# Three expert gathers on one Trainium2 core: down and up rows fetched as one 8 KB row, with weights made row by row

## The reference, cut to what matters

```
def _peer(h, w_pq, peer_keys, peer_down, peer_up):
    q = (h @ w_pq).reshape(B, L, 8, 2, 128)
    s = einsum("blhpd,hpkd->blhpk", q, peer_keys)          # 128 keys per half
    sv, si = lax.top_k(s, 16)
    cand = sv[..., 0, :, None] + sv[..., 1, None, :]       # 256 candidates a head
    top_s, pos = lax.top_k(cand.reshape(..., 256), 16)
    eidx = ...                                             # one of 16384 experts
    gate = softmax(top_s)
    # per block of 128 tokens: 8 heads x 16 = 128 experts a token
    a   = einsum("tkd,td->tk", peer_down[eidx], h)
    act = gate * gelu(a)
    out = einsum("tk,tkd->td", act, peer_up[eidx])
```

## Time and profile before

| | us |
|---|---|
| median of 3 runs | 4169.66 |
| lowest, highest | 4167.23, 4174.44 |
| span of the profiled execution | 4362.9 |
| first gather in it (four tiles) | 447 to 2089 |
| second gather (two tiles) | 2232 to 3065 |
| third gather (two tiles) | 3605 to 4353 |

### The profile page before, as it was taken

How to read it: one execution, slowest core, us unless ns; L and a number is a source line. 1 busy time by engine, 2 the same in 40 slices (tenths; PEclk the granted TensorE clock), 3 DMA queues, 4 the chain that set the end, 5 groups by cost and what they waited for, 6 DMA issues and landing times.

```text
span 4362.9 us, 35889 instructions
## 1 busy us (share of the span) xinstructions
PE 3358.4 (77%) x11238; PEld 1715.0 (39%) x11238; DVE 2577.2 (59%) x5454; ACT 816.5 (19%) x1926; POOL 2040.9 (47%) x2148
## 2 busy tenths in 40 slices
PE   6889686888767787887687766766878887866766
PEld 2357442356434243551354422221366654422111
DVE  1412768566686846676357674666563347684776
ACT  1311111321211122121211111111231211111111
POOL 0210566655555666666116665566000005676665
PEclk9999899999979899996899988866988998999556
DMA  6663998999999999999849999999400039999999
GB/s 228 227 237 130 338 363 320 375 356 409 401 362 355 343 378 352 392 410 375 298 159 369 333 365 392 372 405 374 157 1 1 1 113 338 352 350 372 379 369 346
DMA packets 380787, 1330.31 MB, mean 305 GB/s; under 512 B 39500, under 2 KB 44876, under 8 KB 377016
## 3 DMA queue, kind: packets, MB, share of 16 engines
q0 software_dynamic: 313344, 1141.10, 69.3%
q1 hardware_dynamic: 61104, 164.18, 10.1%
q10 hardware_dynamic: 6152, 22.74, 1.4%
HBM read 1326.69 MB, written 1.17 MB: 304 GB/s over the span
## 4 chain that ended last, share of the span: by engine, by line
PE 15%; DVE 10%; DMA 9%; issue 7%; POOL 5%; another core or an unknown queue 3%; ACT 2%; ACTq 0%; DVEq 0%; POOLq 0%
PE ps L1701 15%; POOL arena L3075 5%; DMA arena<-in_peer_up,arena 5%; DVE arena L893 3%; DVE arena L906 3%; DMA arena<-in_peer_v,arena 2%; ACT arena L2462 1%; DMA arena<-in_ada_w 1%; DMA arena<-in_peer_u,arena 1%; DMA arena<-in_peer_down,arena 1%; PE ps L1707 1%; DVE arena L914 1%; DVE arena L1287 1%; DVE arena L1282 0%
## 5 line engine op out<-in xcount | busy, mean ns | idle before, releaser
L1701 PE MATMUL ps<-arena 128*128 128x512 f32 (+9 forms) x10500 | 3254.6, 490 | 873.9 <-ACT arena L2462 231.9
L1701 PEld LDWEIGHTS ps<-arena 128*128 128x128 f32 (+4 forms) x10500 | 1621.6, 196 | 2435.2 <-issue 1844.2
L906 DVE SCALAR_TENSOR_TENSOR arena<-arena,ps 128x1024 f32<-128x1024 f32 x1024 | 1240.6, 1217 | 542.1 <-DMA arena<-in_peer_down,arena 289.1
L3075 POOL DMA_INDIRECT arena<-in_peer_down,arena x768 | 747.1, 973 | 654.8 <-DVE arena L910 269.5
L3075 POOL DMA_INDIRECT arena<-in_peer_up,arena x768 | 736.5, 959 | 541.2 <-PE ps L1701 294.3
L2462 ACT ACTIVATE arena<-arena 128x128 f32<-128x128 f32 (+5 forms) x1242 | 444.4, 387 | 1890.8 <-PE ps L1701 636.3
L3075 POOL DMA_INDIRECT arena<-in_peer_u,arena x256 | 248.4, 970 | 647.9 <-DVE arena L910 543.6
L906 DVE SCALAR_TENSOR_TENSOR ps<-arena,ps 128x512 f32<-128x512 f32 x508 | 383.4, 755 | 143.0 <-DMA arena<-in_peer_up,arena 88.8
L2462 ACT ACTIVATE arena<-ps 128x512 f32<-128x512 f32 (+4 forms) x349 | 191.5, 549 | 1165.6 <-PE ps L1701 547.9
L3075 POOL DMA_INDIRECT arena<-in_peer_v,arena x256 | 242.4, 947 | 149.2 <-issue 59.9
L893 DVE TENSOR_TENSOR arena<-arena 128x512 f32<-128x512 f32 (+8 forms) x398 | 246.9, 620 | 72.1 <-ACT arena L2462 42.1
(11 more groups left out here) (34 smaller groups left out, 565.1 us busy)
## 6 DMA issues: line engine op xcount, KB each, us to landing
arena<-in_w_mod POOLq DMA_DIRECT2D x40, 1024.0 KB, 6.6
arena<-in_gate_blocks SPq DMA_DIRECT2D x16, 2048.0 KB, 7.8
arena<-in_w_in SPq DMA_DIRECT2D x14, 2048.0 KB, 7.9
arena<-in_w_pq SPq DMA_DIRECT2D x13, 2048.0 KB, 16.0
arena<-in_ada_w POOLq DMA_DIRECT2D x24, 1024.0 KB, 8.3
arena<-in_w_out SPq DMA_DIRECT2D x8, 2048.0 KB, 8.0
arena<-in_gate_blocks SPq DMA_DIRECT2D x8, 1792.0 KB
arena<-mod_scratch ACTq DMA_DIRECT2D x26, 512.0 KB
```

What stands on the lines that cost most here:

```text
L906: self.e.scalar_tensor_tensor(o, a, s, b, op0, op1, accum_out=accum).then_inc(*(inc or self.inc(self.S.vec)))
L1701: return self.e.matmul(o, l, r, start=start, stop=stop)
L3075: self.e.indirect_dma_start(out=o, out_offset=None, in_=table, in_offset=bass.IndirectOffsetOnAxis(ap=idx.bitcast(U32), axis=0)).then_inc( ...
```

## The change

The host lays each table out as one row of 2048 values per expert, down then up. One indirect DMA now fetches both (128 x 8 KB = 1 MB) into one of six pair buffers; the third gather has nine, because memory behind the arena is free by then. The matmul and the DVE's half for a row follow one step behind its dot product (`NEAR` = 1, where `LAG` was 18). Scalar makes the weight of each row by itself: gelu of one column, a Copy that multiplies by the gate, then the diagonal. The DVE's product over 16 columns goes. `fold` works in place in the modulation row and needs no buffer of its own. The layer offset in the expert index goes, since each layer has its own table. Two positions at which other work may go on are rewritten in step numbers (one moves from step 276 to 266, the others stay). To make room, the arena grows and the memory kept for the descriptors of GpSimd's DMAs shrinks from 8192 to 2048 bytes a partition.

```diff
-ND = NU = 5
-GK = 16
-LAG = GK + 2
+NP = 6
+AHEAD = 16
+NEAR = 1
@@ Walk
+    def pair_place(self, s):
+        bufs = self.K.pairs[self.gathers]
+        i = s % len(bufs)
+        return bufs[i], (self.S.pair_in[i], 16 * (self.pair_uses[i] + s // len(bufs) + 1))
@@ main
-            yield ("after", 2 * NEXT + LAG + 2)
+            yield ("after", 2 * NEXT + 10)
@@ Vector.peer_pick
-        if l == 1:
-            self.ts(e0, e0, 16384.0, None, AD, None)
@@ Vector.gather
-                self.stt(d, d, 1.0, K.HP, M, M, inc=self.inc(S.down), free=True, accum=K.AA[n % 2][:, k:k + 1])
-            if s >= GK + 1 and (s - 1) % GK == 0 and s - 1 <= total:
-                ...
-                self.wait_ge(*self.next(S.activated))
-                self.tt(w[:, ks], w[:, ks], K.GT[:, tiles[n_], ks], M, inc=self.inc(S.weighted), free=True)
-            u = s - LAG
+                self.stt(d[:, 0:D], d[:, 0:D], 1.0, K.HP, M, M, inc=self.inc(S.down), free=True, accum=K.AA[n % 2][:, k:k + 1])
+            u = s - NEAR
             if u >= 0:
+                if n % 2:
+                    src, w = self.pair_place(u)[0][:, 1536:2048], K.AW[n % 2][:, k:k + 1]
+                    self.wait_ge(S.weighted, c + 1)
+                    if self.halves(u):
+                        self.wait_ge(S.up_vector, self.halves(u))
+                    ...
+                        self.stt(K.av, src, w, K.av, M, AD, inc=self.inc(S.up_vector), free=True)
@@ Tensor.gather
+            u = s - NEAR
+                buf, there = self.pair_place(u)
+                self.wait_ge(*there)
                 self.wait_ge(S.diagonal, c + 1)
-                ins = self.mm(K.ap, K.dg[c % 4], buf[:, 0:512], k == 0, k == NEXT - 1)
+                ins = self.mm(K.ap, K.dg[c % 4], buf[:, 1024:1536], k == 0, k == NEXT - 1)
                 if n % 2 == 0:
-                    ins = self.mm(K.av, K.dg[c % 4], buf[:, 512:1024], k == 0, k == NEXT - 1)
+                    ins = self.mm(K.av, K.dg[c % 4], buf[:, 1536:2048], k == 0, k == NEXT - 1)
@@ Scalar.gather
-                self.wait_ge(S.down, base + s)
-                self.act(K.AW[n_ % 2][:, ks], K.AA[n_ % 2][:, ks], gelu, inc=self.inc(S.activated))
-                ...
-                self.act(K.dg[c % 4], K.ident, ACT.Copy, scale=K.AW[n % 2][:, k:k + 1], inc=self.inc(S.diagonal), free=True)
+                w = K.AW[n % 2][:, k:k + 1]
+                self.wait_ge(S.down, c + 1)
+                self.act(w, K.AA[n % 2][:, k:k + 1], gelu, inc=self.inc(S.activated), free=True)
+                self.wait_ge(*self.own())
+                self.act(w, w, ACT.Copy, scale=K.GT[:, tiles[n], k:k + 1], inc=self.inc(S.weighted), free=True)
+                self.wait_ge(*self.own())
+                self.wait_ge(S.up_tensor, c - 3)
+                self.act(K.dg[c % 4], K.ident, ACT.Copy, scale=w, inc=self.inc(S.diagonal), free=True)
@@ Pool.gather
-                o, there = self.down_place(s)
-                self.fetch(o, down, K.EI[:, tiles[n], k:k + 1], there[0])
-            u = s - LAG
-                ...
-                o, there = self.up_place(u, total)
-                self.fetch(o, up, K.EI[:, tiles[n], k:k + 1], there[0])
+                self.freed(max(0, s - len(K.pairs[self.gathers]) + 1), total)
+                o, there = self.pair_place(s)
+                self.fetch(o, table, K.EI[:, tiles[n], k:k + 1], there[0])
@@ memory
-    K.NB = NB = 53200
+    K.NB = NB = 54736
-    K.ds, K.us = [gm(D) for _ in range(ND - 1)] + [more(D)], [gm(D) for _ in range(NU - 1)] + [more(D)]
+    common = [gm(2 * D) for _ in range(NP - 1)] + [more(2 * D)]
+    K.pairs = {0: common, 1: common, 2: common + [arena[:, NB - 2 * D * i:NB - 2 * D * (i - 1)] for i in (3, 2, 1)]}
@@ layout
-    f["peer_down"] = np.asarray(inputs["peer_down"]).reshape(2 * 16384, D)
-    f["peer_up"] = np.asarray(inputs["peer_up"]).reshape(2 * 16384, D)
+    f["peer_rows_0"], f["peer_rows_1"] = (np.concatenate([down[i], up[i]], 1) for i in range(2))
@@ kernel
-    nc = bacc.Bacc("TRN2", target_bir_lowering=False, num_devices=1, dynamic_dma_scratch_size=8192)
+    nc = bacc.Bacc("TRN2", target_bir_lowering=False, num_devices=1, dynamic_dma_scratch_size=2048)
```

More of the change, by code:

```diff
@@ L588, in main @@
         zpair = lambda who: K.H2[:, 2 * who:2 * who + 2, 0:928]
[L589 removed]
+        gelu, gelu2 = ACT.Gelu_apprx_tanh, ACT.Gelu
         def temps(mem):
@@ L1346, in peer_topk, with gather @@
         yield from self.peer_pick(l, t, m, 0, 8)
-    def gather(self, tiles, tables, gelu, rows):
+    def gather(self, tiles, table, gelu, rows):
         K, S = self.K, self.S
         base, total = self.base, NEXT * len(tiles)
-        for s in range(total + LAG):
+        for s in range(total + NEAR):
             n, k = divmod(s, NEXT)
@@ L1392, in gather @@
                     self.fold(tiles[n], c, *gate)
-        self.base += total
-        self.shared += total // 2
-        self.gathers += 1
+        self.pairs_done(total)
     def fold(self, t, c, n0, gr, g_in):
@@ L2783, in peer_topk, with gather @@
         yield from self.peer_pick(l, t, m, 0, 8)
-    def gather(self, tiles, tables, gelu, rows):
+    def gather(self, tiles, table, gelu, rows):
         K, S = self.K, self.S
         base, total = self.base, NEXT * len(tiles)
-        for s in range(total + LAG):
+        for s in range(total + NEAR):
             n, k = divmod(s, NEXT)
             yield (tiles[n], k // 32) if s < total and k % 32 == 0 else None
-            if s >= GK and s % GK == 0 and s <= total:
-                n_, g = divmod(s // GK - 1, NEXT // GK)
-                ks = slice(GK * g, GK * g + GK)
-                self.wait_ge(S.down, base + s)
-                self.act(K.AW[n_ % 2][:, ks], K.AA[n_ % 2][:, ks], gelu, inc=self.inc(S.activated))
-            if s < total and k == 0:
-                if base + s:
-                    self.wait_ge(S.down, base + s)
-                self.act(K.HP[:, 0:512], K.H2[:, tiles[n], 0:512], ACT.Copy)
-                self.act(K.HP[:, 512:1024], K.H2[:, tiles[n], 512:1024], ACT.Copy, inc=self.inc(S.row_in_psum))
-            u = s - LAG + 1
-            if 0 <= u < total:
-                n, k = divmod(u, NEXT)
-                c = base + u
-                if k % GK == 0:
-                    self.wait_ge(*self.next(S.weighted))
-                if c >= 4:
-                    self.wait_ge(S.up_tensor, c - 3)
-                self.act(K.dg[c % 4], K.ident, ACT.Copy, scale=K.AW[n % 2][:, k:k + 1], inc=self.inc(S.diagonal), free=True)
-            u = s - LAG
-            if u >= 0 and u % NEXT == NEXT - GK:
@@ L3028, in modhalf, with gather @@
         yield from self.units_of(2)
-    def gather(self, tiles, tables, gelu, rows):
+    def gather(self, tiles, table, gelu, rows):
         K, S = self.K, self.S
-        base, total = self.base, NEXT * len(tiles)
-        down, up = tables
-        for s in range(total + LAG):
+        total = NEXT * len(tiles)
+        for s in range(total + NEAR):
             n, k = divmod(s, NEXT)
```

117 lines of the change are left out of this document (41 added, 76 removed).

## The result

The changed kernel takes 4230.75 us (median; 4225.46 to 4235.75) where the kernel before, timed beside it, takes 4172.05 us (4167.23 to 4176.09): ratio 1.0134, 95% interval 1.0115 to 1.0153. It is 59 us slower. The forecast was 4095 us, 75 faster, and its range ended at 4215.

A forecast was written before the change was run, and what follows sets the result against it. The gathers were taken as bound by DMA, not everywhere at its best rate. Terms 55 + 40 + 20 - 7 - 30 gave 78 us of the 4362.9 us span, 75 unprofiled: 4095 us, range 3985 to 4215.

The forecast's parts named there:

- (1): All gathers: 8 KB packets for 4 KB save 0.06 us a pair, half a fitted line's gain; 55 us gained.
- (2): Third gather: nine pair buffers leave more time for the fetch; 40 us gained; depth unchanged in the first two gathers.
- (3): Start of each gather: pairs carry twice the bytes per dot while down rows were fetched alone before; 20 us gained.
- (4): End of each gather: dot, gelu, weight and diagonal follow the last landing; 7 us lost over three gathers.
- (5): ACT in the first gather: gelu in each row adds table loads around Sigmoids and Exps, mostly hidden; 30 us lost.
- (6): PE's matmul waits for a dot just made, one row behind; taken as unchanged, 0 us.
- Bytes alone count: Rival: 409 GB/s is a byte rate, or 8 KB rows travel as two packets; (1), (2) vanish; about 4175 with loads; chance 0.12.
- The low slices go: Rival: half of what separates the gathers from 409 GB/s may go, 172 us after ends, 4005 us; chance 0.17.
- the second rival: First gather: exposed table loads and doubled PE waiting for ACT outweigh 77 us kept; 147 us lost, 4310 us; chance 0.26.
- (7): Dropped DVE products and index offset, and smaller descriptor memory for GpSimd's modulation loads, cost nothing; 0 us, at most 56 lost.

The follow-up runs named there:

- before_copy: The kernel before with its gelus, one per 16 rows, replaced by Copies: 4175.06 us, 0.9991 of before.
- before_rowweights_copy: The kernel before with expert weights made row by row on ACT, lag of 18 kept, and gelu replaced by Copy: 4205.47 us, 1.0070 of before.
- after_copy_split: The changed kernel with Copy for gelu and each pair fetched by two indirect DMAs of 4 KB rows into the same buffer: 4219.69 us, 1.0094 of before.
- after_copy: The changed kernel with gelu of the expert weights replaced by a Copy: 4164.07 us, 0.9968 of before.
- second profile of before: The kernel before, unchanged, profiled again: 4175.39 us, 0.9995 of before, span 4174.2 us.

## Why the prediction was wrong

A chain of four steps splits the 56 us between before_copy and the changed kernel: weights row by row +30 (before_rowweights_copy), pairs with one row of lag and nine buffers in the third gather +14 (after_copy_split), 8 KB packets -56 (after_copy), gelu's table loads +67 (the changed kernel). The second step also has the rest of the change in it (the fold in place, the smaller descriptor memory), which was not tried alone. The steps were not all timed on one chip; by the ratios to before (0.9991, 1.0070, 1.0094, 0.9968, 1.0134) they are 33, 10, -53 and 69 us. From start to start in the profiles, the first step taken against the second profile of before, the first gather changes by +8, +14, -25 and +68 us, the second by +15, +2, -12 and 0, the third by +8, -7, -16 and +1: together the +65, +5 and -14 of the result.

| step | forecast, us | by the runs, us |
|---|---|---|
| (1) packets | 55 gained | 56 gained |
| (2) depth of nine | 40 gained | 20 gained, 15 of them seen in the third gather |
| (3) fill, (4) ends | 13 gained | not measured alone |
| (5) table loads | 30 lost | 67 lost |
| (6) one row behind, row by row | 0 | 30 lost by weights row by row; pairs and lag lose more, 14 after the 20 of (2) |

(1) Right, as far as the split can tell. That half of the line's gain came out is in part luck: half was a choice between two ends. The pair went from 2.57 to 2.50 us at full rate (half of the way to the 2.44 of the line through the earlier trace rows), and the 8 KB packet takes 316 ns, inside the 320 named. The page of the Trainium skill drawn on, "DMA: Bandwidth & Descriptors", section "Why small descriptors are slow (HBM only)", would have had half of it, 27 us by the estimate made from it; here the packets gave 1.03 times the rate, 420 for 409 GB/s, and the measurement decides. "Bytes alone count" falls with that. Its sum was also off: 17 us lost give about 4186 us with the loads, and not 4175.

(2) The mechanism was right and the size was off by the frame. The time that nine and six buffers leave for the fetch was forecast at 17.1 and 9.5 us; the fetches took 17.2 and 10.2 from issue to landing. But the 92 us that the third gather seemed to lose are mostly those of the one profile; in the second profile of before it is 693 us from its first fetch to the end of the span, and 679 after. "The low slices go" rested on the same rows, and there were none to go. The mark set for (2), a third gather under 715 us, is met by both kernels and tells nothing, and so it is with the 1642 us set for the first: 1600 are below it and still a loss, against the 1535 of the second profile. The windows of the earlier trace rows are also wider than the fetches: the first gather of that profile lasts 1617 us from first fetch to last, and the second 791 where 833 stand.

(3), (4) In the first 32 us of the first gather the rate is 352 GB/s for 339, in the next 401 for 385; that makes 0.9 MB, 2 us, where 7 were counted. Pairs land at over 400 GB/s, the mark set for (3), only for some 10 of the first 32 us (458 to 468 us, slices of 414 to 438). From the last fetch to the end of the span it is 28.3 us for 18.0, but one 1 MB row there stands against one of 512 KB.

(5) The step that failed first. The bound of 83 extra loads counted two for each of 64 foreign functions and no others; 114 came (159 for 45), 146 us at 1.283. And "most of it is hidden by PE's own unit and by buffers that hold several rows" does not hold: 67 of the 146 us are seen in the time, where 30 of 106 were counted. The forecast had the price of a foreign row (3.8 us on ACT), the pace that it competes with (3.2 us a row) and the rival that follows; the rows that lose take 3.6 us. What was misjudged was the weight: at ACT's busy share of 20%, later 46%, the mean hides that where ACT makes each row's weight between the newest dot and the next matmul, a load is in the chain of the buffer. The lag of one row is not the condition for that: with 18 rows kept, and weights row by row, the loads still cost 52 us. The cover that was counted on, PE's own unit, hides the load before a foreign function (4.17 us of waiting are left behind it in the second timeline) and not the load back. And the DMA, whose share was 1.00 in the second profile, has no time in reserve to make it up. The Trainium skill, "ScalarE: Activation LUTs", section "What ACT_TABLE_LOAD costs", has 2.66 us a switch with a drain of 1.38; the timeline above shows loads of 1.28 us, 0.08 and 0.02 us after what stands before them, the Exp 0.01 us and the gelu 0.02 us after them, so a drain is not what made the loads dear.

(6) The second step that failed. "I take it unchanged, because DVE's dots run ahead of PE as far as buffers reach" looked at DVE and not at ACT's own order. Before, ACT needed a new dot once in 16 rows; now it needs one in each, and holds evictions and the next diagonals behind it. Weights row by row cost 30 us by themselves with the lag of 18 kept, and the order is the likely cause (its waits were shown, no run changes it alone). The 0.4 us a row that (5) called "nothing by itself" is the other place where these 30 us were put at nothing. Pairs and the lag of one row cost some 34 more, of which nine buffers give 20 back. PE's wait for ACT rose from 76 to 298 us, over the 230 set as the mark for the second rival. But 246 us of wait stand in after_copy, which is faster than before, so as a mark for the loads it was a poor one; the loss showed in the DMA share of the stretch (0.86 for 0.96).

(7) Right, and for less risk than it named. The 143 us between the first two gathers were read from the windows of the earlier trace rows; from the last fetch to the next gather's first it is 206 us in that profile too, room for 24 loads of 8.3 us even one at a time. The modulation loads land in 6.3 and 8.0 us (page of the changed kernel), as in the earlier trace rows, and the stretch from the first gather's last fetch to the second's first is 207 us in both.

```profile
arena<-in_w_mod POOLq DMA_DIRECT2D x40, 1024.0 KB, 6.3
arena<-in_ada_w POOLq DMA_DIRECT2D x24, 1024.0 KB, 8.0
```

The second rival, "ACT and the short lag set the pace in the first gather", is nearest to what happened, in the milder form named there (4180 to 4310): the loads at 67 us for 106, weights row by row, pairs and lag at some 64 (30, and 14 after the 20 of (2)) for 118, against gains of 76 (56 and 20) for 77. It had a chance of 0.26. It is right for the loads, whose cost lies all in the first gather; of the 64 us only some 22 (8 and 14) lie there, the rest in the other two. Open is how the loss of pairs and lag splits between the lag and the shared buffer in the first gather, where no memory is left for more pairs.

## What to carry to other kernels

Before a stage is split into single rows on an in-order engine, write down what stands behind each new wait on that engine, and put the stage's longest row (table loads included) against the pace of the transfer, stretch by stretch; a busy share of 20% says nothing on that. Count buffers as rows in flight (buffers less those held by the lag), and choose the lag by it: here, with the table loads, two rows were better than one, and three lost 120 us; without the loads one row was best. And before a sum is built on one profile whose span is 4.6% above the timed runs, take no gain from stalls that only it shows.

## What the runs showed of the hardware

An indirect DMA of 128 rows of 8 KB keeps GpSimd busy for 936 ns (median), one of 128 rows of 4 KB for 937 in the second profile of before (941 in the earlier trace rows): twice the bytes cost GpSimd nothing. The count of rows was not varied. Duration min/median/max, first and last start, of the changed kernel:

```profile
L3030 POOL DMA_INDIRECT arena<-in_peer_rows,arena x1024: 932/936/2992, 448.8 to 4202.6; - x171
```

Packets of 8 KB run at 420 GB/s and those of 4 KB at 409, both with the engines' share over 1.00. Some three rows of 1 MB in flight mark the edge: from 2280 to 2950 us the second gather runs at 392 GB/s with 3.4 rows in flight (one row of lag), at 387 with 3.1 (two rows; 223 fetches of 9.2 us) and at 351 with 2.6 (three rows). Fewer rows in flight also follow from a lower rate, so the runs with three rows of lag, where nine buffers kept the pace and six did not, say more than these figures alone.

```profile
2280.00:2950.00 670.00, 490.09 (x1254) 204.68 (x1252) 443.94 (x952) 223.00 (x708) 216.68 (x224) 0.87 0.98 392
2280.00:2950.00 670.00, 481.29 (x1099) 191.59 (x1097) 448.20 (x948) 221.62 (x701) 216.69 (x223) 0.83 0.97 387
2280.00:2950.00 670.00, 489.48 (x1409) 226.97 (x1408) 409.97 (x936) 207.96 (x632) 189.85 (x196) 0.87 0.90 351
```
